# Feed-forward down projection streamed by output columns, with x, its squares and the next norm's input made block by block beside it

## The reference, cut to what matters

```python
def swiglu(h, w_gate, w_up, w_down):
    return (jax.nn.silu(h @ w_gate) * (h @ w_up)) @ w_down

# first stack, per layer (mix and cross attention ahead of this)
h = rms_norm(x, pre_ffn_g[l])
x = x + rms_norm(swiglu(h, w_gate[l], w_up[l], w_down[l]), post_ffn_g[l])

# second stack, per layer
h = rms_norm_2(x, ffn1_norm[l])
x = x + 0.5 * swiglu_2(h, ffn1_w_gate[l], ffn1_w_up[l], ffn1_w_down[l])
h = rms_norm_2(x, mix_norm[l])
...
x = x + merged @ w_out[l]
h = rms_norm_2(x, ffn2_norm[l])
x = x + 0.5 * swiglu_2(h, ffn2_w_gate[l], ffn2_w_up[l], ffn2_w_down[l])
```

## Time and profile before

| | us |
|---|---|
| median of 3 runs | 2480.09 |
| lowest, highest | 2479.8, 2481.58 |
| the profiled execution, device time | 2480.8 |
| its span, first to last instruction | 2478.9 |
| PE busy | 2221.4 (90%) |
| DVE busy | 1430.3 (58%) |
| ACT busy | 1137.6 (46%) |
| mean granted TensorE clock | 0.948 |

### The profile page before, as it was taken

The page is one execution under the profiler, slowest core; times in us unless marked ns, Lnnn a source line. Parts: engine busy times, 40 slices in busy tenths (PEclk is TensorE's granted clock), DMA queues, the critical chain, the costliest instruction groups (busy, mean ns, idle before and its releaser), DMA issues.

```text
span 2478.9 us, 40437 instructions
## 1 busy us (share of the span) xinstructions
PE 2221.4 (90%) x17158; PEld 2126.7 (86%) x17158; DVE 1430.3 (58%) x2194; ACT 1137.6 (46%) x1745; POOL 83.8 (3%) x81
## 2 busy tenths in 40 slices
PE   3888879998988799979998998899999988988999
PEld 2877779998868799979997877899899988878999
DVE  3454656546546565465557556655556575556654
ACT  3354444443545444444445456444444444465442
POOL 4000000000000000010000000000000000000000
PEclk9888899998989999989999899999999998989999
DMA  5632425554423255645644223456456543234554
GB/s 131 188 102 84 137 83 179 186 187 136 131 74 130 96 164 181 204 145 184 200 141 153 86 79 109 158 184 194 150 187 193 165 153 102 86 103 133 176 186 153
DMA packets 97956, 360.28 MB, mean 145 GB/s; under 512 B 11064, under 2 KB 11065, under 8 KB 97264
## 3 DMA queue, kind: packets, MB, share of 16 engines
q1 hardware_dynamic: 95616, 348.17, 43.4%
q0 software_dynamic: 1728, 6.38, 1.3%
q10 hardware_dynamic: 432, 3.15, 0.3%
HBM read 354.25 MB, written 3.41 MB: 144 GB/s over the span
## 4 chain that ended last, share of the span: by engine, by line
PE 74%; DVE 13%; ACT 7%; issue 2%; POOL 2%; DMA 2%; ACTq 0%; DVEq 0%; POOLq 0%
PE bank L259 65%; DVE w_lo L1234 3%; ACT w_hi L779 2%; PE bank L311 1%; POOL sq L1803 1%; DMA raw<-in_stream 1%; PE bank L295 1%; PE bank L639 1%; DVE sq L1287 1%; DVE xn_lo L1260 1%; PE bank L316 1%; DVE x L1291 1%; DVE sq L1771 1%; PE bank L312 1%; ACT sq L790 0%
## 5 line engine op out<-in xcount | busy, mean ns | idle before, releaser
L259 PE MATMUL bank<-xn_hi,w_hi 128*128 128x256 f32 x3296 | 959.1, 291 | 136.6 <-DVE xn_lo L1260 103.9
L1234 DVE TENSOR_TENSOR w_lo<-raw,w_hi 128x1024 fp32r<-128x1024 f32 x664 | 809.9, 1252 | 470.1 <-ACT w_hi L779 469.9
L259 PE MATMUL bank<-xn_lo,w_hi 128*128 128x256 f32 x3296 | 950.2, 288 | 0.0
L259 PE MATMUL bank<-xn_hi,w_lo 128*128 128x256 f32 x3296 | 949.1, 288 | 0.0
L779 ACT ACTIVATE w_hi<-raw 128x1024 fp32r<-128x1024 f32 x664 | 674.2, 1050 | 339.2 <-PE bank L259 321.0
L259 PEld LDWEIGHTS bank<-xn_hi,w_hi 128*128 128x128 f32 x3296 | 651.4, 198 | 151.7 <-issue 137.7
L259 PEld LDWEIGHTS bank<-xn_lo,w_hi 128*128 128x128 f32 x3296 | 651.4, 198 | 0.2
L259 PEld LDWEIGHTS bank<-xn_hi,w_lo 128*128 128x128 f32 x3296 | 650.6, 197 | 0.0
L259 PE MATMUL bank<-hid_hi,w_hi 128*128 128x256 f32 x1056 | 291.5, 276 | 0.0
L259 PE MATMUL bank<-hid_lo,w_hi 128*128 128x256 f32 x1056 | 291.5, 276 | 0.0
L259 PE MATMUL bank<-hid_hi,w_lo 128*128 128x256 f32 x1056 | 291.5, 276 | 0.0
(11 more groups left out here) (338 smaller groups left out, 2562.8 us busy)
## 6 DMA issues: line engine op xcount, KB each, us to landing
raw<-in_stream SPq DMA_DIRECT2D x664, 512.0 KB, 4.2
skew<-logit POOLq DMA_DIRECT2D x1, 2304.0 KB, 35.2
table<-skew POOLq DMA_DIRECT2D x1, 1408.0 KB, 7.4
logit<-in_small POOLq DMA_DIRECT2D x4, 288.5 KB, 3.1
con<-in_con ACTq DMA_DIRECT2D x1, 1029.0 KB, 7.1
xn<-in_mem ACTq DMA_DIRECT2D x1, 1024.0 KB, 11.6
x<-in_x ACTq DMA_DIRECT2D x1, 1024.0 KB, 14.9
out<-x POOLq DMA_DIRECT2D x1, 1024.0 KB, 4.2
```

Of the source, the lines that this page charges most:

```text
L259: m = T.matmul(out, a, b, start=first and j == 0, stop=True, skip_group_check=True)
L1234: V.tensor_tensor(w_lo[m % RING], raw[m % RING], w_hi[m % RING].bitcast(F32), ALU.subtract).then_inc(*lo_done.next())
```

## The change

**The stream.** `lay_out` cuts the down matrix by 256 output columns, all 22 hidden tiles of a column block behind each other (88 hidden-by-output tile pairs in 11 slots as before). A half now holds four hidden tiles for one bank. Bank b is complete after 22(b+1)/4 halves: 5.5, 11, 16.5 and 22 of the 22 halves. `down_end(f, b)` is the wait for it. DOWN_DONE is [2, 5, 8, 10], the slots in which the banks end. The count of matmuls, of slots and of bytes is the same.

**Beside the down slots** ACT and DVE do, behind their splits `ahead` of slots 2, 5 and 8, the work of pairs 0, 1 and 2: in the second stack x, xn_hi, squares and (one step later) xn_lo of the next norm, in the first stack the squares of the banks and their sums. Pair 3 stays behind the last slot.

**Beside wo1 to wo3** the same is done for pairs 0 to 2 of the second stack's mixer output. For that the operand of wo moves from xn_hi, xn_lo to `merged_in_hi`, `merged_in_lo`, which start where hid_hi starts (`base`).

**New small parameters** of the next layer are copied in its predecessor's last feed-forward.

**Not touched:** POOL's program, SP's, the gate and up slots, what follows the first stack's mean.

```diff
+DOWN_DONE = [(FT * (b + 1) - 1) // KT for b in range(4)]
...
+    merged_in_hi, merged_in_lo = (sb_at(f"merged_{n}", [P, KT, S], F32R, base + at) for n, at in (("hi", 0), ("lo", 8192)))
...
+    def down_end(f, b):
+
+        if b % 2 == 0:
+            return down_made.at(2 * f + b // 2 + 1)
+        return half_used.at(2 * SLOT_AT[(f, "down", 0)] + FT * (b + 1) // HK)
...
-            for j in range(FB - 1):
-                for k, r in halves((f, "down", j)):
-                    for ct in range(KT):
-                        m = down_tile(j, k, r, ct, j == 0)
+            for j in range(FB):
+                for half, r in halves((f, "down", j)):
+                    for part in range(HK):
+                        b, k = divmod((2 * j + half) * HK + part, FT)
+                        if (b, k) == (0, FT - 2):
+                            T.wait_ge(*hid_made.at(FB * f + FB))
+                        for ct in range(2):
+                            m = products(acc[b][:, ct, :], tile(r, part, slice(ct * P, (ct + 1) * P)),
+                                         [t[:, k, :] for t in (hid_hi, hid_lo)], k == ct == 0)
+                        if b % 2 == 0 and k == FT - 1:
+                            m.then_inc(*down_made.next())
...
-                slot_T(at(f"wo{b}"), acc[b], xn_hi, xn_lo, second=merged.at(4 * l + 4) if b == 0 else None)
+                slot_T(at(f"wo{b}"), acc[b], merged_in_hi, merged_in_lo, second=merged.at(4 * l + 4) if b == 0 else None)
...
             for j in range(FB):
                 ahead((f, "down", j))
+                if j in DOWN_DONE[0:3]:
+                    beside(DOWN_DONE.index(j))
...
+            beside = next_in(3 * L + 2, small_2("ffn2"))
             for b in range(4):
                 ahead(at(f"wo{b}"))
-            AC.wait_ge(*slot_end(at("wo3")))
-            ffn(DEPTH + 2 * l + 1, 3 * L + 2, small_2("ffn2"), norm_no(L, 2))
+                if 1 <= b:
+                    beside(b - 1)
...
+            def next_in(i, gain, update):
+                def pair(b):
+                    if b:
+                        in_pair(i, gain, b - 1)
                     update(b)
-            new_small(L)
...
+                return pair
...
-        for j in range(FT // 2):
-            put(pair(down[2 * j * P:2 * (j + 1) * P]))
+        by_columns = np.concatenate([pair(down[:, c:c + COLS]) for c in range(0, D, COLS)], 1)
+        for j in range(FB):
+            put(by_columns[:, j * SLOT:(j + 1) * SLOT])
```

More of the change, by code:

```diff
@@ L813, in norm_add @@
             load_sqrt()
-            for b in range(4):
+            for b in sorted(ready):
                 AC.wait_ge(*ready[b])
@@ L1269, in norm_scale, with norm_add @@
             V.wait_ge(*own.last())
-        def norm_add(n, gain, scaled=False):
+        def norm_add(n, gain, scaled=None):
+            add_squares(n, range(3 if scaled else 1, 4))
             if scaled:
-                V.scalar_tensor_tensor(root[:, 1, :], root[:, 0, :], EPS, root[:, 0, :], ALU.mult, ALU.mult).then_inc(*own.next())
-            add_squares(n)
-            if scaled:
-                V.wait_ge(*own.last())
+                V.wait_ge(*scaled)
                 V.wait_ge(*mean_made.at(n + 1))
@@ L1293, in norm_add, with ffn @@
             return update
-        def ffn(f, i, gain, update):
+        def ffn(f, i, gain, update, done, beside):
             def silu(j):
@@ L1308, in hidden @@
                          hid_hi_made.at(FB * f + j + 1), hid_made)
-            norm_in(i, gain, update)
+            norm_in(i, gain, update, done)
             ahead((f, "gate", 0))
@@ L1321, in ffn @@
                 ahead((f, "down", j))
+                if j in DOWN_DONE[0:3]:
+                    beside(DOWN_DONE.index(j))
         def half_update(f):
[L1325 removed]
             def update(b):
[L1328 removed]
+                V.wait_ge(*down_end(f, b))
                 V.scalar_tensor_tensor(sq[:, pair_of(b), :], acc[b], 0.5, scale_2, ALU.mult, ALU.mult).then_inc(*own.next())
@@ L1784, in add, with last_pair @@
                 V.tensor_tensor(x[:, pair_of(b), :], x[:, pair_of(b), :], acc[b], ALU.add).then_inc(*x_updated.next())
-            ffn(DEPTH + 2 * l + 1, 3 * L + 2, small_2("ffn2"), add)
-            update = half_update(DEPTH + 2 * l + 1)
-        for b in range(4):
-            update(b)
+            beside = next_in(3 * L + 2, small_2("ffn2"), add)
+            for b in range(4):
+                ahead(at(f"wo{b}"))
+                if 1 <= b:
+                    beside(b - 1)
+            last = half_update(DEPTH + 2 * l + 1)
+            def last_pair(b):
+                if l + 1 == DEPTH:
+                    last(b)
+                else:
+                    if b == 0:
+                        second_small(L + 1)
+                    next_in(3 * (L + 1), small_2("ffn1"), last)(b)
+            ffn(DEPTH + 2 * l + 1, 3 * L + 2, small_2("ffn2"), add, 3, last_pair)
+        last(3)
     def pool_program():
```

134 lines of the change are left out of this document (75 added, 59 removed).

## The result

| | us |
|---|---|
| changed kernel, median of 4 | 2452.5 (2451.3 to 2453.6) |
| kernel before beside it, median of 4 | 2480.0 (2479.7 to 2481.6) |
| ratio, 95% interval | 0.9888 (0.9871 to 0.9905) |
| profiled execution after: device time, span | 2452.9, 2451.1 |

The change saves 27.5 us where 30.2 were forecast, and 2452.5 lies inside the range; the two profiled spans differ by 27.8. Lines of the code have moved: L259 is now L270, the mean L295 is L306, the low part L1260 is L1283, the update L1329 and L1331 is L1360 and L1362, the split L1234 is L1261, POOL's add L1803 is L1869.

The account below looks back on a forecast made before the run. PE, busy 2221.4 of 2478.9 us, was taken as the bound, leaving its idle time and slow clock to gain. 19.2 behind the down slots, 10.0 behind wo and 1.0 for wo's rate make 30.2: 2480.1 to 2450 us, range 2441 to 2464.

Parts of the forecast that it names:

- Inside the down slots: Down slots: the rate follows the moving tile, so matmuls stay at 0.113 us and the new order costs nothing.
- the rival's price: Down slots: the rival that order sets the rate, at 0.120 us a matmul, giving back 21.2 us (2471); chance 0.10.
- What hides the moved work: Beside down slots: moved work costs nothing; half 8's split ends at E + 5.2 (E: bank 0's end), 1.6 us to spare.
- Behind the down slots: Three second-stack places: end of PE's work to mean of squares falls to 6.3 us, gaining 4.6, 4.6 and 7.7.
- Behind wo: Two places from wo3 into feed-forward 2: end of PE's work to mean falls to 6.4 us, gaining 4.6 and 5.4.
- POOL can't begin ahead of T0: Layer 0 behind wo: POOL waits for wo3's end (T0, the end of PE's work) to fetch parameters; 6.4 us taken there.
- The clock behind the first place, 2.3: Feed-forward 1 into mixer, layer 0: 26 matmuls behind M (start of the mean of squares) regain full clock, 2.3 us.
- wo's rate, 1.0: wo slots: the moved operand takes matmuls from 0.120 to 0.113 us, counted as 1 us for both layers.
- fell to 1.2 GHz: Five places: the rival that idles of 0.7 to 1.3 us lower the clock, costing 11.5 us (2461); chance 0.10.
- the five places: Second-stack waits for xn_lo the change touches: two feed-forward 1 into mixer, two wo3 into feed-forward 2, one into next layer.
- the sign to look for: Profile after, five places: PE should wait about 0.7 to 1.3 us for xn_lo, just ahead of the second half.
- fourth rival: Ahead of wo and in the mixer: two further 1.2 GHz stretches vanish, M behind wo at 5.8; 2442 us, chance 0.07.

Follow-up runs that it names:

- e3: Changed kernel with the shared region (hid, wo's operand, mem) starting 64 bytes higher: 2477.8 us, ratio 0.9976 to the kernel before.
- e8: Changed kernel with the second stack's pair work behind the down slots again, in the order of the kernel before: 2473.0 us, ratio 0.9956 to the kernel before.
- e7: Changed kernel with pads putting split weights at 64 modulo 128 bytes and all other big tiles at 0: 2440.3 us, ratio 0.9828 to the kernel before.
- e4: Changed kernel without the 64 spare bytes behind the shared region, so every big tile starts at 0 modulo 128: 2476.4 us, ratio 0.9979 to the kernel before.
- e11: Changed kernel with the addresses of e7, POOL's fetch behind its adds, and beside wo each update ahead of the previous pair's low part: 2439.3 us, ratio 0.982.
- e2: Changed kernel with pairs 0 to 2 of the mixer output behind wo3 instead of beside wo: 2459.2 us, ratio 0.9907 to the kernel before.

## Why the prediction was right, and where a term was off

- **Inside the down slots: right.** 179 matmuls in 20 us, 60.0 us each, no wait for w_lo. The reason given, the moving tile, was half of it: it is where the moving tile lies against the weights. Had hid been on w's offset, 21 us would have been lost, as e3 shows; the rival's price was right and its cause (the order) wrong.
- **What hides the moved work: right.** The 1.6 us to spare behind bank 0 measured 1.8 to 2.1 (one copy free, two not), and the split of half 8 ended at E + 5.2, as counted. Only bank 0's cover was tried; those of banks 1 and 2 are known just from PE not waiting there.
- **Behind the down slots: right.** 6.4 for 6.3 three times; gains 4.5, 7.6 and 4.5 for 4.6, 7.7 and 4.6.
- **Behind wo: the mis-sized term.** Forecast 4.6 + 5.4, measured 3.0 + 5.0. Layer 1 is within 0.4. In layer 0 the step "POOL can't begin ahead of T0, since its own program waits for the end of wo3" was read as sparing DVE, and failed: the squares of two pairs had piled up by then, and their adds fell on the last pair's chain, 1.5 us on one low part. The experiment with the later fetch gives back 1.25 us of the 1.6 that this place fell short. It moves the issue of the fetch along with the adds, so it does not tell the two apart; the rows point at the adds.
- **The clock behind the first place, 2.3: right, and too small.** It gave 3.2 us, since the whole low stretch behind M went (6.83 us of it); the forecast priced 26 matmuls of it. With the pairs behind the down slots again (e8) it came back.
- **wo's rate, 1.0: right.** wo ran at 0.1133 in both layers once past its first halves, which is about 0.8 us a layer, an estimate from 120 matmuls at 0.0067 each.
- **What the forecast left out, and luck.** The two mixers with wo changed by -5.6 and +2.9. The 3.2 and 0.8 above leave about -1.6 in layer 0 and +3.7 in layer 1, which moved with the granted clock: the 60 matmuls around the start of wo took 14.6 us before and 12.1 after in layer 0, 12.2 and 14.6 in layer 1. That the mixers come to 2.7 us where 2.3 + 1.0 were forecast is therefore luck. A forecast can carry this only as width, some 3 us a mixer; the range did.
- **The rivals.** No place of the changed kernel fell to 1.2 GHz with waits of 0.6 to 2.2 us. Waits of 1.8 and 2.2 us in two of the experiments were followed by it, so the length of one gap alone does not decide. POOL released no mean at the five places. At the second of them PE waited 2.21 us, where the sign to look for was 0.7 to 1.3. The prediction's fourth rival, more clock coming back, came true in layer 0 and was undone in layer 1.

## What to carry to other kernels

Work moved beside a stream is free up to the cover, which can be counted from rows (bank's end, chain, next split), and an order that is harmless under cover costs 1.1 us a pair without it. A helper engine that is held back by an unrelated wait can later burst into the critical chain, as POOL did here; moving the unrelated wait freed 1.25 us at that place, though the whole did not get faster by more than the intervals can tell. Where TensorE is the bound, print the offsets of weights and moving tiles and try them apart: two pads of 64 bytes gave 12 to 15 us here (e7, by time and by ratio), about as much as the whole overlap beside the down slots.

## What was not expected of the hardware

- **The spacing of 256-column matmuls depends on two addresses.** Weights and moving tile on one offset modulo 128 bytes: 0.1200 us. 32 apart: 0.1183 with hid moving, 0.1200 with xn. 64 apart: 0.1133 or 0.1178. The Trainium skill, TensorE: Matmul & The Clock Gate, section "Step-by-step: what each phase is for", gives PE two independent read ports and says that loading weights takes nothing from a running matmul. That is hard to square with e3, e4 and e7, which differ from the changed kernel in nothing but offsets: by up to 0.0067 us a matmul, and by 22 to 37 us of the kernel, reckoned from the ratios of e3 and e4 against those of the changed kernel and e7.
- **Two spacings with the same addresses**, each kept over a whole down part of 528 matmuls (e7, e11), and seen in the wo slots of e2 and e8 too. What switches them stays open.
- **A mixer stage takes 297 to 307 us** in kernels that differ mostly elsewhere, with mean granted clocks of 0.91 to 0.95, and yet the same to 0.1 us in two profiles of one kernel, and in e3 and e4, which share their spacings. That points at the kernel's own timing; what in it places the falls stays open, and a difference of 3 us between two single profiles of different kernels is not a finding.
